# Gate and up products with high and low parts of the activations in one 512-column matmul

## The chip, the cores and the metric

The kernel runs on one core of one Trainium2 chip. The metric is the device time of one execution in microseconds (us), lower is better. Three runs of the kernel before took 1592.2, 1594.12 and 1595.83 us; their median is 1594.12 us.

## What is computed

The reference runs two small transformers one after the other on 256 tokens of width 1024. The first has two layers, each with a mixer (retention, sparse attention, a spatial gating unit) and a gated feed-forward block (FFN) of width 2816. The second has two layers with other mixers (HGRN2 with an S5 scan, latent attention) and an FFN whose gate passes a causal convolution over three tokens. Cut to the FFNs, which the change touches:

```python
# first block, both layers
gate, up = jnp.split(h @ w_gate_up[l], 2, axis=-1)
x = x + (jax.nn.silu(gate) * up) @ w_down[l]

# second block, both layers (conv over 3 tokens, per channel, plus bias)
a, u = jnp.split(hn @ w_in, 2, axis=-1)
a = conv(a, conv_w) + conv_b
return (jax.nn.silu(a) * u) @ w_out
```

All inputs are fp32.

## The kernel before

**Number format.** Most large products are made from two parts of each operand: a high part, which is the value rounded to the type fp32r (a copy by ScalarE), and a low part, which is the rest (a subtraction by VectorE). `mm3` (L512) issues three matmuls for each pair of 128x128 weights and moving columns: high x high (L514), high x low (L515) and low x high (L516), all accumulated in one place. `hTh` and `hTl` are the two parts of the normed activations, turned so that the model dimension lies on the partitions: 128 x 8 contraction blocks x 256 tokens.

**Weights.** SyncE loads weight pieces of 1 MB (2048 elements per partition) into three slots `wraw`. ScalarE writes the high part of a piece into one of three pairs `wpair` (`split_high`, L1107), VectorE the low part (`split_low`, L1624). A pair is written again when TensorE has finished with it, and a `wraw` slot is loaded again when the low part is made.

**FFN.** There are four, called by `tag` 0 to 3 below (tags 2 and 3 have the convolution). Each has 22 chunks of 128 hidden channels, two chunks in each of 11 steps. TensorE (`ffn`, L573) does in a step: `gate_up` of two chunks, and `down` of the step before. `gate_up` (L580) takes one of the four PSUM banks `work` for a chunk, gate in columns 0 to 255 and up in 256 to 511: 2 halves x 8 contraction blocks x 3 matmuls of 256 columns with the weights as stationary operand. `down` (L592) issues 24 matmuls of 512 columns into the four banks `accum`, with `hidh` and `hidl` (the two parts of the hidden activations) as stationary operand.

**ScalarE in a step** (L1149 to L1174): one split; for each chunk Silu from PSUM (L1160), or scale and bias for the convolution (L1162) and later Silu (L1166); a second split; the high parts of the hidden activations (L1172); a third split. **VectorE in a step** (L1677 to L1696): one split; for tags 2 and 3 the two other taps of the convolution, read from PSUM (L1684, L1686); the product of gate and up, with up read from PSUM (L1690), which frees the bank; a second split; the low parts of the hidden activations (L1694); a third split. Each engine works through its list in this order, waiting on semaphores.

**Beside it.** In FFN 1 GpSimd also computes the tables of the S5 scan (from L1459; the large operations are at L1544 to L1555), which are needed later. `rows` (L226) is a buffer of 128 x 2 x 1024 that no FFN uses before the final norm, except that the norms before an FFN write squares to it.

## Time and profile before

| | |
|---|---|
| median of three runs | 1594.12 us |
| span of the profiled execution | 1593.6 us |
| TensorE matmuls, busy | 1439.2 us (90%), 8688 matmuls |
| TensorE weight loads, busy | 1258.2 us (79%) |
| VectorE busy | 856.6 us (54%) |
| ScalarE busy | 618.1 us (39%) |
| GpSimd busy | 199.5 us (13%) |
| DMA | 212.06 MB, 133 GB/s on average |

The profile is one execution. Its span runs from the first to the last instruction. Busy time of an engine counts its instructions, not its waits; matmuls overlap in their pipeline, so that the sum of their durations is more than their share of the clock on the wall, and the distance between two starts is what one costs in a stream. PE is TensorE's matmuls, PEld its weight loads, DVE VectorE, ACT ScalarE, POOL GpSimd, SP SyncE. A line such as L514 is a line of the kernel. In a row, `out<-in` are the tensors written and read, and `<-` behind an idle time names what ended it.

### The profile page before, as it was taken

The page shows a single profiled execution, that of the slowest core. Times are in us where ns is not written, and L with a number is a line of the kernel's source. Part 1 is how long each engine was busy: PE and PEld are TensorE (multiplying, and loading weights), DVE is VectorE, ACT ScalarE, POOL GpSimd, SP SyncE. Part 2 cuts the span into 40 slices and gives each one's busy share as a digit, 9 for nine tenths or more (in the row PEclk, how much of TensorE's full clock was granted, in tenths as well). Part 3 has the DMA queues.
Part 4 walks back from the last instruction along what each step waited for, and adds up shares of the span by engine and source line. Part 5 has one row for each costly group of instructions (what it writes and reads, how often), then busy time and mean ns, then how long its engine had stood idle before and what let it go on. Part 6 is the DMA issues. An engine that isn't in the chain of part 4 may idle for free.

```text
span 1593.6 us, 20677 instructions
## 1 busy us (share of the span) xinstructions
PE 1439.2 (90%) x8688; PEld 1258.2 (79%) x8688; DVE 856.6 (54%) x1016; ACT 618.1 (39%) x835; POOL 199.5 (13%) x210
## 2 busy tenths in 40 slices
PE   6699999999999989799998894498999989899998
PEld 5588678999978767699997882268999876699997
DVE  4263525444456254344568658936566635466555
ACT  3322424433443233255433451025445425354543
POOL 0010000000001010004897004400000000000000
PEclk9886569999999655899999997689999999999999
DMA  7542114665543301455665330054665524456561
GB/s 251 168 121 78 32 48 141 182 187 185 181 156 80 121 27 53 93 155 181 181 190 168 108 105 0 1 159 132 197 186 174 186 67 148 115 148 184 171 198 67
DMA packets 257532, 212.06 MB, mean 133 GB/s; under 512 B 26222, under 2 KB 220031, under 8 KB 257440
## 3 DMA queue, kind: packets, MB, share of 16 engines
q1 hardware_dynamic: 244266, 206.91, 42.6%
q10 hardware_dynamic: 13174, 3.83, 1.4%
q8 instruction: 69, 1.13, 0.3%
q14 instruction: 23, 0.19, 0.0%
HBM read 208.10 MB, written 2.62 MB: 132 GB/s over the span
## 4 chain that ended last, share of the span: by engine, by line
PE 78%; DVE 10%; DMA 3%; ACT 3%; issue 2%; SPq 1%; ACTq 1%; POOL 1%; DVEq 0%; POOLq 0%
PE work L514 10%; PE accum L514 10%; PE work L516 10%; PE work L515 10%; PE accum L515 10%; PE accum L516 10%; DMA wraw<-in_w_in 3%; DVE wpair L1624 2%; PE accum L813 2%; PE work L782 2%; DVE arena L2059 2%; PE work L690 1%; PE work L564 1%; ACT wpair L1107 1%; PE work L793 1%
## 5 line engine op out<-in xcount | busy, mean ns | idle before, releaser
L1624 DVE TENSOR_TENSOR wpair<-wraw,wpair 128x2048 fp32r<-128x2048 f32 (+1 forms) x187 | 439.2, 2351 | 414.3 <-ACT wpair L1107 414.2
L1107 ACT ACTIVATE wpair<-wraw 128x2048 fp32r<-128x2048 f32 (+1 forms) x187 | 355.3, 1901 | 383.0 <-PE work L516 156.4
L514 PE MATMUL work<-hTh,wpair 128*128 128x256 f32 x1408 | 399.0, 283 | 5.9 <-DVE hTl L1632 4.9
L516 PE MATMUL work<-hTh,wpair 128*128 128x256 f32 x1408 | 398.2, 283 | 0.0
L515 PE MATMUL work<-hTl,wpair 128*128 128x256 f32 x1408 | 398.2, 283 | 0.0
L514 PEld LDWEIGHTS work<-hTh,wpair 128*128 128x128 f32 x1408 | 269.8, 192 | 8.1 <-DVE hTl L1632 6.5
L515 PEld LDWEIGHTS work<-hTl,wpair 128*128 128x128 f32 x1408 | 269.8, 192 | 2.7 <-issue 1.1
L516 PEld LDWEIGHTS work<-hTh,wpair 128*128 128x128 f32 x1408 | 269.9, 192 | 0.0
L514 PE MATMUL accum<-wpair,hTh 128*128 128x512 f32 (+2 forms) x416 | 169.6, 408 | 29.7 <-DVE wpair L1624 19.3
L1445 POOL TENSOR_SCALAR rs<-ss 128x1 f32<-128x1 f32 (+5 forms) x29 | 7.0, 241 | 1285.5 <-ACT rows L1097 919.2
L515 PE MATMUL accum<-wpair,hTh 128*128 128x512 f32 (+2 forms) x416 | 167.0, 401 | 0.0
L516 PE MATMUL accum<-wpair,hTl 128*128 128x512 f32 (+2 forms) x416 | 166.7, 401 | 0.0
L514 PE MATMUL accum<-wpair,hidh 128*128 128x512 f32 x352 | 140.2, 398 | 7.4 <-DVE hidl L1694 5.8
L515 PE MATMUL accum<-wpair,hidh 128*128 128x512 f32 x352 | 140.1, 398 | 0.0
L516 PE MATMUL accum<-wpair,hidl 128*128 128x512 f32 x352 | 140.1, 398 | 0.0
L514 PEld LDWEIGHTS accum<-wpair,hTh 128*128 128x128 f32 x416 | 86.5, 208 | 50.1 <-issue 20.7
L516 PEld LDWEIGHTS accum<-wpair,hTl 128*128 128x128 f32 x416 | 86.4, 208 | 16.3
L515 PEld LDWEIGHTS accum<-wpair,hTh 128*128 128x128 f32 x416 | 86.8, 209 | 15.2
L514 PEld LDWEIGHTS accum<-wpair,hidh 128*128 128x128 f32 x352 | 66.9, 190 | 23.0 <-DVE wpair L1624 8.5
L516 PEld LDWEIGHTS accum<-wpair,hidl 128*128 128x128 f32 x352 | 66.6, 189 | 16.1
L515 PEld LDWEIGHTS accum<-wpair,hidh 128*128 128x128 f32 x352 | 66.7, 190 | 14.3
L564 PE MATMUL work<-diag,x 128*128 128x128 f32 x256 | 40.3, 327 | 25.8 <-DVE diag L1636 25.6
(356 smaller groups left out, 1721.3 us busy)
## 6 DMA issues: line engine op xcount, KB each, us to landing
wraw<-in_w_gate_up SPq DMA_DIRECT2D x88, 512.0 KB, 5.1
wraw<-in_ffn_w_in SPq DMA_DIRECT2D x88, 512.0 KB, 5.0
wraw<-in_w_in SPq DMA_DIRECT2D x24, 1024.0 KB, 5.2
wraw<-in_w_down SPq DMA_DIRECT2D x22, 1024.0 KB, 4.9
wraw<-in_ffn_w_out SPq DMA_DIRECT2D x22, 1024.0 KB, 4.9
wraw<-in_even_w_in SPq DMA_DIRECT2D x10, 1024.0 KB, 5.2
wraw<-in_w_out SPq DMA_DIRECT2D x8, 1024.0 KB, 6.4
wraw<-in_even_w_out SPq DMA_DIRECT2D x4, 1024.0 KB, 5.1
```

What stands on the lines that cost most here:

```text
L514: mm(dst, still[0], move[0], start=start, stop=False)
L515: mm(dst, still[0], move[1], start=False, stop=False)
L516: return mm(dst, still[1], move[0], start=False, stop=stop)
L564: i = mm(b[:, k * P:(k + 1) * P], x[:, t, c:c + P], diag[:, t, :], start=True, stop=True)
L690: i = mm(b[0:HD, j * 32:j * 32 + 30], w1[:, k, :], blk[:, j, k, :], start=(k == 0), stop=(k == CMP_LEN - 1))
L782: i = mm(b[:, br * T:br * T + K], qTn[r, q, t * P:(t + 1) * P], kTn[r, br, 0:K], start=True, stop=True)
L793: i = tr(b[:, c:c + P], probs[n % 4][:, br * T + k * P:br * T + (k + 1) * P], ident[:])
L813: i = mm(banks[1 + br][:, e], pT[:, n % 3, (br * (t + 1) + k) * P:(br * (t + 1) + k + 1) * P], proj[:, k, c:c + HD], start=(k == 0), stop= ...
L1107: fn(W.pair(k)[0], W.source(k), ACT.Copy).then_inc(S["w_high"], 1)
L1445: ts(rs[0:parts, c0:c0 + n], ss[0:parts, c0:c0 + n], 1.0 / width, EPS, ALU.mult, ALU.add).then_inc(own, 1)
L1624: tt(lo, W.source(k), hi, ALU.subtract).then_inc(S["w_low"], 1)
L2059: i = v.tensor_tensor_scan(z[:, j, :], f, w[:, j, :], 0.0, ALU.mult, ALU.add)
```

## The change

The two parts of the activations now lie next to each other in one tensor `hT`, so that for one contraction block high and low parts are 512 neighbouring columns. For each chunk and half, one matmul of 512 columns multiplies the high weights with both parts (high x high into columns 0 to 255 of the bank, high x low into columns 256 to 511), and one of 256 columns adds low weights x high activations into columns 0 to 255. Each half of a chunk takes a bank of its own. VectorE then sums the two halves of each bank with a `tensor_reduce` into SBUF, the gate into `graw` and the up product into `uraw`, both views of `rows`, and that frees the bank. ScalarE, the convolution and the product read `graw` and `uraw` from there. The high parts of the hidden activations wait for a semaphore `hid_made` of their own.

```diff
-        hTh = sb("hTh", [P, KC, T], F32R)
-        hTl = sb("hTl", [P, KC, T], F32R)
+        hT = sb("hT", [P, KC, 2, T], F32R)
+        hTh, hTl = hT[:, :, 0, :], hT[:, :, 1, :]
+        graw = rows[:, 0, :].rearrange("p (f n) -> p f n", f=4)
+        uraw = rows[:, 1, :].rearrange("p (f n) -> p f n", f=4)
...
                 def gate_up(f):
 
-                    pe.wait_ge(*wk.turn())
-                    b = wk.fill(("gu", tag, f))
                     pe.wait_ge(*W.parts(("gu", tag, f)))
                     w = [m.rearrange("p (c h n) -> p c h n", c=KC, h=2) for m in W.pair()]
                     for h in range(2):
+                        pe.wait_ge(*wk.turn())
+                        b = wk.fill(("gu", tag, f, h))
                         for c in range(KC):
-                            i = mm3(b[:, h * T:(h + 1) * T], [m[:, c, h, :] for m in w], hT_at(c, slice(0, T)), c == 0, c == KC - 1)
-                    i.then_inc(*wk.fills(("gu", tag, f)))
-                    W.used(*wk.filled(("gu", tag, f)))
+                            hT_at(c, slice(0, T))
+                            mm(b, w[0][:, c, h, :], hT[:, c].rearrange("p k n -> p (k n)"), start=(c == 0), stop=False, skip_group_check=True)
+                            i = mm(b[:, 0:T], w[1][:, c, h, :], hTh[:, c, :], start=False, stop=(c == KC - 1), skip_group_check=True)
+                        i.then_inc(*wk.fills(("gu", tag, f, h)))
+                    W.used(*wk.filled(("gu", tag, f, 1)))
...
                     for f in chunks:
-                        act.wait_ge(*wk.filled(("gu", tag, f)))
-                        b = wk.bank(("gu", tag, f))
+                        act.wait_ge(*wk.freed(("gu", tag, f, 0)))
                         if f >= 4:
                             act.wait_ge(S["hid_ready"], FC * tag + f - 3)
                         if tag < 2:
-                            fn(sg[:, f % 4, :], b[:, 0:T], ACT.Silu).then_inc(S["act_silu"], 1)
+                            fn(sg[:, f % 4, :], graw[:, f % 4, :], ACT.Silu).then_inc(S["act_silu"], 1)
                         else:
-                            fn(sg[:, f % 4, :], b[:, 0:T], ACT.Identity, scale=v[:, 44 + f:45 + f], bias=v[:, 66 + f:67 + f]).then_inc(S["conv_in"], 1)
+                            fn(sg[:, f % 4, :], graw[:, f % 4, :], ACT.Identity, scale=v[:, 44 + f:45 + f], bias=v[:, 66 + f:67 + f]).then_inc(S["conv_in"], 1)
...
                     for f in chunks:
-                        act.wait_ge(*wk.freed(("gu", tag, f)))
+                        act.wait_ge(S["hid_made"], ln.next(S["hid_made"]))
...
                     split_low(1)
+                    for f in chunks:
+                        dve.wait_ge(*wk.filled(("gu", tag, f, 0)))
+                        b = wk.bank(("gu", tag, f, 0))
+                        v.tensor_reduce(graw[:, f % 4, :], b.rearrange("p (k n) -> p n k", k=2), AX_X, ALU.add).then_inc(*wk.frees(("gu", tag, f, 0)))
+                        dve.wait_ge(*wk.filled(("gu", tag, f, 1)))
+                        b = wk.bank(("gu", tag, f, 1))
+                        v.tensor_reduce(uraw[:, f % 4, :], b.rearrange("p (k n) -> p n k", k=2), AX_X, ALU.add).then_inc(*wk.frees(("gu", tag, f, 1)))
                     if tag >= 2:
                         for f in chunks:
-                            c, b = sg[:, f % 4, :], wk.bank(("gu", tag, f))
+                            c, b = sg[:, f % 4, :], graw[:, f % 4, :]
...
                     for f in chunks:
-                        b = wk.bank(("gu", tag, f))
                         dve.wait_ge(S["act_silu"], ln.next(S["act_silu"]))
-                        tt(sg[:, f % 4, :], sg[:, f % 4, :], b[:, T:2 * T], ALU.mult).then_inc(*wk.frees(("gu", tag, f)))
+                        dve.wait_ge(*wk.freed(("gu", tag, f, 1)))
+                        tt(sg[:, f % 4, :], sg[:, f % 4, :], uraw[:, f % 4, :], ALU.mult).then_inc(S["hid_made"], 1)
```

## Rows read from the trace of the kernel before

**Rows 1.** The page: busy time and share of each engine, and the chain's shares.
```profile
PE 1439.2 (90%) x8688; PEld 1258.2 (79%) x8688; DVE 856.6 (54%) x1016; ACT 618.1 (39%) x835; POOL 199.5 (13%) x210
...
PE 78%; DVE 10%; DMA 3%; ACT 3%; issue 2%; SPq 1%; ACTq 1%; POOL 1%; DVEq 0%; POOLq 0%
```

**Rows 2.** Busy time in FFNs 0 to 3 and the end of FFN 1.
```profile
252.00:443.00 191.00, 189.95 (x1330) 177.11 (x1328) 95.81 (x85) 78.39 (x81) 0.00 (x0) 1.00 0.58 177
675.00:843.00 168.00, 165.53 (x1184) 155.73 (x1183) 92.02 (x74) 78.02 (x84) 99.90 (x123) 1.00 0.59 175
1082.00:1268.00 186.00, 184.59 (x1309) 172.89 (x1307) 112.07 (x125) 89.08 (x103) 0.00 (x0) 1.00 0.58 174
1395.00:1587.00 192.00, 190.33 (x1331) 177.52 (x1330) 113.09 (x130) 88.05 (x103) 0.74 (x2) 1.00 0.52 154
860.00:877.00 17.00, 12.61 (x50) 9.81 (x49) 13.69 (x11) 3.70 (x5) 9.29 (x8) 0.90 0.75 247
```
The columns of rows 2 are: stretch, its length, then busy us (and instructions) of PE, PEld, DVE, ACT and POOL, the granted clock (1 is full), the busy share of the DMA engines and their GB/s.

**Rows 3.** Groups by line, shapes apart: busy us, mean ns, idle before.
```profile
L1624 DVE TENSOR_TENSOR wpair<-wraw,wpair 128x2048 fp32r<-128x2048 f32 x184 | 434.9, 2365 | 413.7 <-ACT wpair L1107 413.5
L514 PE MATMUL work<-hTh,wpair 128*128 128x256 f32 x1408 | 399.0, 283 | 5.9 <-DVE hTl L1632 4.9 <-issue 1.1
...
L1690 DVE TENSOR_TENSOR sg<-sg,work 128x256 f32<-128x256 f32 x88 | 36.4, 416 | 35.1 <-ACT sg L1160 30.6 <-ACT sg L1166 4.6
...
L1644 DVE TENSOR_TENSOR sg<-work,vecs 128x512 f32<-128x512 f32 x32 | 22.1, 691 | 14.0 <-PE work L564 13.4
...
L1917 DVE TENSOR_REDUCE arena<-arena 128x2 f32<-128x512 f32 x12 | 8.2, 686 | 0.4
```

**Rows 4.** Timeline of TensorE, a step of FFN 3: start us, duration us.
```profile
1455.10 0.39 PE L514 MATMUL accum<-wpair,hidh 128*128 128x512 f32 x1
...
1460.71 0.28 PE L514 MATMUL work<-hTh,wpair 128*128 128x256 f32 x1
...
1472.22 0.39 PE L514 MATMUL accum<-wpair,hidh 128*128 128x512 f32 x1
```

**Rows 5.** Timeline of TensorE, input projection of layer 0.
```profile
84.98 0.39 PE L514 MATMUL accum<-wpair,hTh 128*128 128x512 f32 x1
...
87.93 0.39 PE L515 MATMUL accum<-wpair,hTh 128*128 128x512 f32 x1
```

**Rows 6.** Timelines of ScalarE, then VectorE, in the same step of FFN 3.
```profile
1449.60 1.92 ACT L1107 ACTIVATE wpair<-wraw 128x2048 fp32r<-128x2048 f32 x1 [3.83 <-PE work L516]
...
1457.26 1.90 ACT L1107 ACTIVATE wpair<-wraw 128x2048 fp32r<-128x2048 f32 x1
...
1451.55 2.29 DVE L1624 TENSOR_TENSOR wpair<-wraw,wpair 128x2048 fp32r<-128x2048 f32 x1 [3.45 <-ACT wpair L1107]
...
1455.90 0.48 DVE L1684 SCALAR_TENSOR_TENSOR sg<-work,vecs,sg 128x255 f32<-128x255 f32 x1 [1.15 <-ACT sg L1162]
...
1459.19 2.29 DVE L1624 TENSOR_TENSOR wpair<-wraw,wpair 128x2048 fp32r<-128x2048 f32 x1 [1.39 <-ACT wpair L1107]
```

**Rows 7.** Timeline of TensorE at the end of FFN 2, first matmuls of two down products.
```profile
1262.23 0.39 PE L514 MATMUL accum<-wpair,hidh 128*128 128x512 f32 x1
...
1269.43 0.47 PE L514 MATMUL accum<-wpair,hidh 128*128 128x512 f32 x1 [1.43 <-DVE hidl L1694]
```

**Rows 8.** Lines L1690 and L1694: duration ns minimum/median/maximum, first and last start.
```profile
L1690 DVE TENSOR_TENSOR sg<-sg,work x88: 406/414/423, 264.7 to 1577.2; 128x256 f32<-128x256 f32 x88
...
L1694 DVE TENSOR_TENSOR hidl<-sg,hidh x88: 410/419/4847, 270.7 to 1578.1; 128x256 fp32r<-128x256 f32 x88
```

**Rows 9.** Timelines of GpSimd, VectorE and TensorE at the end of FFN 1.
```profile
819.32 1.91 POOL L1550 TENSOR_TENSOR arena<-arena 128x1024 f32<-128x1024 f32 x1
...
842.66 6.72 POOL L1548 TENSOR_TENSOR arena<-arena 128x2048 f32<-128x2048 f32 x1
...
844.81 8.60 DVE L1694 TENSOR_TENSOR hidl<-sg,hidh 128x256 fp32r<-128x256 f32 x2
...
869.36 0.47 PE L514 MATMUL accum<-wpair,hidh 128*128 128x512 f32 x1 [4.39 <-DVE hidl L1694]
```

More of the change, by code:

```diff
@@ L439, in build @@
           cmp_scores cmp_exp cmp_probs cmp_turned gates_ready gm_rows silu_ready mixed
-          act_silu hid_high hid_ready down_done conv_in conv_done
+          act_silu hid_made hid_high hid_ready down_done conv_in conv_done
           s5_dt s5_arg s5_trig lb_arg lb_exp s5_tables s5_pad s5_wT table_done
```

## Prediction, made before the changed kernel was run

> **What bounds the kernel now.** I read the page's busy shares and its chain first. TensorE is busy for 90% of the span and holds 78% of the chain that ended last [rows 1], so TensorE is the first suspect. The stretches of the four feed-forward blocks (FFNs), cut out of the span, sharpen this: in each, TensorE is busy for over 98% of the stretch at full granted clock, while VectorE is busy for 50 to 60% [rows 2]. The groups by line say what the time is: 1408 matmuls of each of the three kinds of the gate and up product, 256 columns each [rows 3]. Their 283 ns of mean duration overlap, so a duration is not a cost here. The cost is the distance from start to start, and it is read from the timeline. In FFN 3, 24 down matmuls of 512 columns lie between 1455.10 and 1460.71, and 96 gate-up matmuls of 256 columns between 1460.71 and 1472.22 [rows 4]: 5.61/24 = 233.8 ns and 11.51/96 = 119.9 ns, with no gap. So one step of an FFN (two chunks and one down product) is 17.1 us of unbroken TensorE work, and what shortens a matmul there shortens the span, as long as VectorE and ScalarE keep up.
>
> **Part 1: two matmuls become one.** For each chunk, half and contraction block, three matmuls of 256 columns (359.7 ns) become one of 512 and one of 256. The number of columns is the same, so only what a matmul costs beside its columns is saved. For 512 columns the trace has two prices. The down product pays 233.8 ns [rows 4]. The input projection of layer 0 runs 13 distances between 84.98 and 87.93 [rows 5], 226.9 ns each. I take 226.9, because those matmuls use the same two tensors as the changed ones (hTh and wpair), while the down product has hidh and hidl as stationary operand; at 256 columns nothing suggests that it matters which of the two tensors moves. The new pair is then 226.9 + 119.9 = 346.8 ns, 12.9 ns less; with the down product's price it is 353.7 ns, 6.0 ns less. There are 1408 triples, 352 per FFN: 18.2 us in all, 4.5 per FFN, or at the other end 8.5 and 2.1. A third of these weight loads goes too, but they lie beside the matmuls already and I cost them at nothing.
>
> **Part 2: VectorE sums the halves.** Added are 4 reduces a step, 176 in all, each reading 512 elements per partition from PSUM. No such form is in the trace. The nearest is the reduce of 512 elements in SBUF, 686 ns [rows 3]. From below, a 128x256 operation with a PSUM input is 414 ns [rows 3], if output elements counted instead of input elements. From above, twice the nearest row, 1.37 us, if the stride of 256 elements between the two summed values halves the read rate. I take 0.69 us, 0.63 from start to start as neighbours overlap: 2.5 us a step. Nothing is saved against it: the product at L1690 stays, with an SBUF operand.
>
> Where do they go? They stand behind the first weight split of the step and in front of everything else, and four waits for filled banks stand there; the convolution, the products, the second split and the low parts of hid queue behind them. Take the end of the first chunk as t = 0, from the step in FFN 3 [rows 6]. ScalarE's high part of the split starts at 0.3 us and VectorE's low part ends at 4.5. The reduces run 4.5 to 7.0 (the fourth needs only the second chunk, which ends at 5.55). The convolutions, twice 0.48 us a chunk and 1.0 with the wait between them, end at 9.0, the last Silu at 9.4, the second split's high part (1.9) at 11.3, its low part (2.3) at 13.5. TensorE needs that pair when the second chunk of the next step starts, at 5.55 + 5.61 + 5.55 = 16.7. Slack 3.2 us, so in the steady state I cost the reduces at nothing; that cover is gone when one reduce takes over 0.63 + 3.2/4 = 1.4 us. In FFNs 0 and 1 there is no convolution and the slack is about 5.7 us. The banks (four, now two per chunk) are free at 5.1 to 7.0, before TensorE comes back to them at 11.2. The third split (down weights) ends at about 16.5, needed at 22.3. SyncE's loads follow the splits by up to 2 us later than now; each has over 5 us before its split.
>
> **Part 3: the ends of the FFNs.** After the last chunk only one down product (5.6 us) covers the chain, not three. In FFN 2 that chain already ends last: the last chunk ended at 1262.23 and the last down product began at 1269.43, after a wait of 1.43 us for hidl [rows 7], 7.2 us after. With the reduces, the fourth ends 1.4 us after the chunk, both convolutions come behind it, hidh's high parts wait for the later product, and hidl comes at about 8.8: 1.6 us more. In FFN 0 without a convolution hidl comes at 6.2 against 5.6 needed, but the additions behind it are held by the last split as now: 0.1 us. In FFN 3 no splits are left, hidl comes at 5.2: nothing.
>
> **Part 4: FFN 1, where GpSimd works too.** This is the largest unknown. The product at L1690 now reads one operand from PSUM and takes 406 to 423 ns in all 88 cases; hidl's subtraction at L1694 reads two from SBUF, takes 419 in the median, and once 4847 [rows 8]. That one began at 844.81, under a GpSimd table operation that began at 842.66 and ran for 6.72 us, and two of them took 8.60 us; TensorE then waited 4.39 us for hidl at 869.36 [rows 9]. After the change the product reads sg and uraw, both in SBUF, so in FFN 1 two more VectorE operations a step can be caught like this. The table operations of 2048 elements lie in the last two steps only. There I laid the order out anew: split, reduces, product behind one GpSimd operation, the next product behind the next one (about 4.4 us each when not held itself: 6.72 less the 2.3 us of the split that was in front), then split, two subtractions. The split for the last chunk ends some 5.5 us after TensorE wants it, the low part of that step's hid and its down weights come at about 863.7, the last down product starts near 872 against 869.36 now. After such waits the granted clock is below full (0.90 in that stretch [rows 2]), which adds up to 1.5 us. So FFN 1 gives back its 4.5 us and ends about 2 us later than now. Bounds: if the products slip between the table operations, the 4.5 us stay; if each catches a further one, it ends 6 us later.
> The Trainium skill states the same as a rule (SBUF — State Buffer, Who interferes with whom): a VectorE operation with two SBUF inputs contends with GpSimd, and whoever holds the shared port blocks the other, while a reduce on this chip never does. The 4847 ns agree; that the reduces stay free, no run here shows. Without the rule FFN 1 would save its 4.5 us.
>
> **Sum.** FFN 0: -4.5 + 0.1. FFN 1: +2. FFN 2: -4.5 + 1.6. FFN 3: -4.5. Together -9.8 us on the profiled span of 1593.6, so 1583.8. The median of the runs shown, 1594.12, is 0.5 us above that span, so the forecast is 1584.3.
>
> **The rivals.**
> A. The 512-column matmul costs here what it costs in the same step, 233.8 ns. For: the down product stands beside it, with the same ScalarE, VectorE and DMA activity. Against: the operands differ, and the projections run at 226.9. It gives FFN 0 -2.0, FFN 1 +3, FFN 2 -0.5, FFN 3 -2.1: -1.6, 1592.5.
> The Trainium skill (TensorE: Matmul & The Clock Gate, Back-to-back issue gap) gives N/2.4 + 2.5 ns for an isolated stream, so that a merged pair would save 2.5 ns: 3.5 us in all as an estimate of that page, near rival A. The trace does not agree, as its 256 columns take 119.9 ns and not 109.
> B. Slower: the reduce reads PSUM so slowly that it ends last. From 1.4 us each, what is above it is paid four times in each of the 20 steps of FFNs 2 and 3. At three times the nearest row (2.06 us) that is 2.6 us x 20 = 53 us, less the 10 saved: about 1637. Against: an operation on 128x512 with a PSUM input takes 691 ns, no more than the reduce from SBUF [rows 3].
> C. GpSimd and VectorE catch each other in more than the last two steps of FFN 1, from which hid and splits come late by 3 us a step in the five steps with wide table operations: +15 on FFN 1 instead of +2, 1597.3. Against: before the last two steps the table operations are half as long or less (1.91 us for one of 1024 elements [rows 9]), and the slack is 5.7 us.
> D. The products slip through, FFN 1 saves 4.5 us: 1577.8.
>
> **How the numbers follow.** Forecast 0.57 (1580 to 1588), A 0.19, B 0.05, C 0.07, D 0.12. What a measurement can tell from no change is about 0.2%, 3.2 us. Forecast and D are faster: 0.69. A is the same, with a part of it either side: 0.18. B, C and a rest of A are slower: 0.13. The range takes in D and A with the profile's scatter: 1577 to 1595, leaving out B, C and the far ends.
>
> **What would show it.** The timeline inside a chunk: distances of 227 and 120 ns alternating (forecast), or 234 and 120 (A). The reduce's mean: 0.69 us; no wait of TensorE for wpair in FFNs 0, 2 and 3. In FFN 2 the wait for hidl grows from 1.4 to about 3 us, less with slower matmuls. In FFN 1 L1690's successor has a maximum of several us, and TensorE waits for a split before the last chunk. If that product never exceeds 0.5 us, part 4 is wrong; if TensorE waits in every step of FFNs 2 and 3, part 2 is.

## The result, and the profile after

The changed kernel took 1591.18 us (median of 20 runs) beside 1595.78 us of the kernel before (20 runs, on the same chip): ratio 0.9963, 95% interval 0.9945 to 0.9981, so 5.9 us faster, with 3.0 to 8.8 in the interval. That is faster by more than the 0.2% that can be told from no change. The forecast was 9.8 us, the range holds the measured time, and the size is off: the forecast's 9.8 lie beyond the interval's end.

The page of the changed kernel (the lines that answer to [rows 1] and [rows 3]; the groups read busy us, mean ns, idle before):

```profile
span 1585.4 us, 18125 instructions
PE 1432.2 (90%) x7280; PEld 1185.3 (75%) x7280; DVE 963.0 (61%) x1192; ACT 627.2 (40%) x835; POOL 200.0 (13%) x210
L591 PE MATMUL work<-hT,wpair 128*128 128x512 f32 x1408 | 497.0, 396 | 9.7 <-DVE hT L1635 5.7
L592 PE MATMUL work<-hT,wpair 128*128 128x256 f32 x1408 | 395.3, 281 | 0.0
L1686 DVE TENSOR_REDUCE rows<-work 128x256 f32<-128x512 f32 x88 | 59.9, 681 | 0.0
L1689 DVE TENSOR_REDUCE rows<-work 128x256 f32<-128x512 f32 x88 | 59.8, 679 | 0.0
```

L591 is the merged matmul, L592 the 256-column one that is left, L1686 and L1689 are the sums. TensorE has 1408 matmuls fewer and is as busy as before in share, so it still sets the pace. Where did the time go? The four FFNs, from the start of the first gate-up matmul to the start of the last down matmul, in the profile of the changed kernel:

```profile
252.16:438.21 186.05, 185.26 (x967) 157.28 (x968) 120.04 (x127) 79.98 (x81) 0.00 (x0) 1.00 0.60 181
669.45:868.27 198.82, 189.12 (x967) 159.69 (x968) 150.77 (x127) 88.53 (x92) 125.83 (x133) 0.98 0.57 172
1075.55:1264.02 188.47, 185.26 (x968) 157.11 (x968) 139.67 (x171) 93.97 (x107) 0.20 (x2) 1.00 0.59 180
1392.14:1577.69 185.55, 185.04 (x968) 157.35 (x968) 135.26 (x169) 89.70 (x102) 0.26 (x2) 1.00 0.52 159
```

The columns are those of rows 2. Cut in the same way, the kernel before has 188.97, 198.21, 190.63 and 188.97 us. So FFN 0 gained 2.9 us, FFN 1 lost 0.6, FFN 2 gained 2.2, FFN 3 gained 3.4: 7.9 in all. The stages between the FFNs differ too, by 4.3 us less to 6.0 us more, though no instruction of theirs was edited: between FFN 0 and FFN 1 the profiles of the kernel before and of the four kernels below that keep three matmuls show 231.0 to 237.0 us, those of the nine with the merged one 228.2 to 232.9 (means 234.3 and 230.2). If those 4 us belonged to the change in every run, the timed gain would be near 12 us, and its interval ends at 8.8. What they are stays open. Below, I compare the sum of the four FFNs, beside the timed ratio.

What a pair costs is read from the start of a step's gate-up product to the start of the down product behind it, 32 pairs. Two steps of FFN 0 in a row:

```profile
297.78 0.40 PE L591 MATMUL work<-hT,wpair 128*128 128x512 f32 x1
308.89 0.39 PE L516 MATMUL accum<-wpair,hidh 128*128 128x512 f32 x1
314.51 0.39 PE L591 MATMUL work<-hT,wpair 128*128 128x512 f32 x1
325.80 0.40 PE L516 MATMUL accum<-wpair,hidh 128*128 128x512 f32 x1
```

11.11/32 = 347.2 ns in the first, 11.29/32 = 352.8 ns in the second. These are close to the two sums that the prediction had as alternatives (346.8 and 353.7), and they take turns, step by step, in all four FFNs; the down product always pays 5.62/24 = 234 ns. Nothing waits in these steps. Within a pair the split is another than forecast: from the start of a 512-column matmul to the next start it is 230.1 ns on average in the first product shown and 236.2 in the products at the high price, and behind the 256-column one 116.9 and 116.5. So no pair is 227 + 120 or 234 + 120; only the pair's sum is.

Which step gets which price is not fixed by the program. The gate-up product of FFN 0 that took 11.11 us above took 11.29 in the kernel below with the tables two steps earlier, which differs from the changed one only in when ScalarE does some work of FFN 1:

```profile
299.49 0.39 PE L591 MATMUL work<-hT,wpair 128*128 128x512 f32 x1
310.78 0.40 PE L516 MATMUL accum<-wpair,hidh 128*128 128x512 f32 x1
```

The two prices took turns in all four FFNs of all six profiled kernels that keep the changed kernel's matmuls, their order and the place of their operands (the changed one, and of those below the sum in PSUM, the wide operations left out, the tables earlier, the doubling in halves and the doubling moved).

The end of FFN 1 in the changed kernel: TensorE, then VectorE, then GpSimd (brackets: idle us before, and what ended it; "x2" is two operations shown as one row).

```profile
842.76 0.50 PE L591 MATMUL work<-hT,wpair 128*128 128x512 f32 x1 [3.95 <-DVE wpair L1627]
853.46 0.50 PE L516 MATMUL accum<-wpair,hidh 128*128 128x512 f32 x1 [3.30 <-DVE wpair L1627]
862.82 0.47 PE L516 MATMUL accum<-wpair,hidh 128*128 128x512 f32 x1 [1.93 <-DVE hidl L1704]
...
830.89 6.20 DVE L1700 TENSOR_TENSOR sg<-sg,rows 128x256 f32<-128x256 f32 x2
837.01 5.69 DVE L1627 TENSOR_TENSOR wpair<-wraw,wpair 128x2048 fp32r<-128x2048 f32 x1
842.63 8.55 DVE L1704 TENSOR_TENSOR hidl<-sg,hidh 128x256 fp32r<-128x256 f32 x2
...
832.12 4.68 POOL L1551 TENSOR_TENSOR arena<-arena 128x2048 f32<-128x2048 f32 x1
836.89 3.67 POOL L1553 TENSOR_TENSOR arena<-arena 128x2048 f32<-128x2048 f32 x1
840.64 5.54 POOL L1555 TENSOR_TENSOR arena<-arena 128x2048 f32<-128x2048 f32 x1
```

VectorE's operations with two SBUF operands wait for the GpSimd operation that runs and then take their own time: the pair of products, about 0.4 us each elsewhere, takes 6.20 us and ends at 837.09, after L1551 has ended at 836.80; the split, 2.29 us elsewhere, takes 5.69 and ends 2.1 us after L1553. Three waits of TensorE stand beside them, 9.2 us. The kernel before had two, 6.0 us: 4.39 for hidl [rows 9] and this one for a split:

```profile
859.09 0.50 PE L514 MATMUL accum<-wpair,hidh 128*128 128x512 f32 x1 [1.62 <-DVE wpair L1624]
```

The splits were thus held in the kernel before already: two in a row took 5.70 and 6.70 us there, from 853.34 on. And the last down product of FFN 1, which comes behind the last wait, ran at a lower granted clock (the number in front of the DMA share) in the kernel before and at the full one in the changed kernel, which hides 1.5 us (first the kernel before, then the changed one):

```profile
869.36:876.35 6.99, 6.99 (x23) 5.57 (x24) 3.69 (x4) 1.15 (x2) 0.20 (x2) 0.76 0.98 333
862.82:868.27 5.45, 5.45 (x23) 4.40 (x24) 3.91 (x4) 1.22 (x3) 0.20 (x2) 1.00 0.95 283
```

### The profile page after: what moved, and what is told of

Its sections match the earlier page's. It is cut to its first block, busy times and chain, and to the rows that moved or that the text cites. A ratio compares the mean times of both kernels' runs of the same rounds, so it can differ in the third digit from the quotient of the medians.

```text
span 1585.4 us, 18125 instructions
## 1 busy us (share of the span) xinstructions
PE 1432.2 (90%) x7280; PEld 1185.3 (75%) x7280; DVE 963.0 (61%) x1192; ACT 627.2 (40%) x835; POOL 200.0 (13%) x210
## 3 DMA queue, kind: packets, MB, share of 16 engines
HBM read 208.10 MB, written 2.62 MB: 133 GB/s over the span
## 4 chain that ended last, share of the span: by engine, by line
PE 78%; DVE 11%; DMA 3%; ACT 3%; issue 2%; ACTq 1%; POOL 1%; SPq 0%; DVEq 0%; POOLq 0%
PE work L591 19%; PE accum L516 10%; PE accum L517 10%; PE accum L518 10%; PE work L592 10%; DMA bias_line<-arena 3%; PE accum L817 2%; DVE wpair L1627 2%; PE work L786 2%; DVE arena L2069 2%; ACT wpair L1111 1%; PE work L566 1%; PE work L694 1%; PE work L797 1%; PE accum L810 1%
## 5 line engine op out<-in xcount | busy, mean ns | idle before, releaser
L1627 DVE TENSOR_TENSOR wpair<-wraw,wpair 128x2048 fp32r<-128x2048 f32 (+1 forms) x187 | 434.8, 2327 | 360.8 <-ACT wpair L1111 360.6
L591 PE MATMUL work<-hT,wpair 128*128 128x512 f32 x1408 | 497.0, 396 | 9.7 <-DVE hT L1635 5.7
L592 PE MATMUL work<-hT,wpair 128*128 128x256 f32 x1408 | 395.3, 281 | 0.0
L591 PEld LDWEIGHTS work<-hT,wpair 128*128 128x128 f32 x1408 | 264.7, 188 | 73.9 <-DVE hT L1635 7.8
L592 PEld LDWEIGHTS work<-hT,wpair 128*128 128x128 f32 x1408 | 266.7, 189 | 1.6
L516 PE MATMUL accum<-wpair,hT 128*128 128x512 f32 (+2 forms) x416 | 171.4, 412 | 25.6 <-DVE wpair L1627 15.3
L517 PE MATMUL accum<-wpair,hT 128*128 128x512 f32 (+2 forms) x416 | 168.2, 404 | 0.0
L518 PE MATMUL accum<-wpair,hT 128*128 128x512 f32 (+2 forms) x416 | 167.7, 403 | 0.0
L516 PEld LDWEIGHTS accum<-wpair,hT 128*128 128x128 f32 x416 | 87.0, 209 | 46.6 <-issue 14.7
L518 PEld LDWEIGHTS accum<-wpair,hT 128*128 128x128 f32 x416 | 87.2, 210 | 16.6
L517 PEld LDWEIGHTS accum<-wpair,hT 128*128 128x128 f32 x416 | 87.5, 210 | 15.7
L1686 DVE TENSOR_REDUCE rows<-work 128x256 f32<-128x512 f32 x88 | 59.9, 681 | 0.0
L1689 DVE TENSOR_REDUCE rows<-work 128x256 f32<-128x512 f32 x88 | 59.8, 679 | 0.0
```

Of the source, the lines that this page charges most:

```text
L516: mm(dst, still[0], move[0], start=start, stop=False)
L517: mm(dst, still[0], move[1], start=False, stop=False)
L518: return mm(dst, still[1], move[0], start=False, stop=stop)
L591: mm(b, w[0][:, c, h, :], hT[:, c].rearrange("p k n -> p (k n)"), start=(c == 0), stop=False, skip_group_check=True)
L592: i = mm(b[:, 0:T], w[1][:, c, h, :], hTh[:, c, :], start=False, stop=(c == KC - 1), skip_group_check=True)
L1627: tt(lo, W.source(k), hi, ALU.subtract).then_inc(S["w_low"], 1)
```

## The experiments

All are timed beside the kernel before; a difference in us is the ratio's, on 1598 to 1599 us. "FFNs" is the sum of the four stretches above in the profile (before 766.8, changed 758.9).

**The merged matmul alone taken back.**

```diff
-mm(b, w[0][:, c, h, :], hT[:, c].rearrange("p k n -> p (k n)"), start=(c == 0), stop=False, skip_group_check=True)
+mm(b[:, 0:T], w[0][:, c, h, :], hTh[:, c, :], start=(c == 0), stop=False, skip_group_check=True)
+mm(b[:, T:2 * T], w[0][:, c, h, :], hTl[:, c, :], start=False, stop=False, skip_group_check=True)
```

> The change without its one merged matmul: bank per half chunk, the sums on VectorE and all its waits stay as in the changed kernel, but each triple is again three matmuls of 256 columns (high x high, high x low, low x high), so each costs 3 x 119.9 = 359.7 ns instead of 346 to 355 ns. Theory M (the merged matmul alone carries the gain, TensorE bounds the FFNs): the gate and up products take 11.5 us in a step again, 1408 x about 9.6 ns = 13.5 us more than the changed kernel, which was 5.9 us below the kernel before; so about 7.6 us above the kernel before, ratio 1.005, and no step of FFN 0, 2 or 3 under 17.1 us. Rival V (the change gains by its banks and its sums, which free or fill something earlier, or VectorE sets the pace): within 2 us of the changed kernel, ratio 0.995 to 0.998.

Measured: ratio 1.0049 (1.0025 to 1.0073), 7.8 us above the kernel before; FFNs 771.6. A step's gate-up product takes 11.50 us again:

```profile
299.54 0.28 PE L591 MATMUL work<-hT,wpair 128*128 128x256 f32 x1
311.04 0.39 PE L516 MATMUL accum<-wpair,hidh 128*128 128x512 f32 x1
```

Theory M holds: 7.8 us for 7.6, closer than the interval (4.0 to 11.7) can show. The merged matmul brings 12.7 us in the FFNs (771.6 less 758.9) and 13.7 in time by the two ratios; everything else in the change costs 4.8 in the FFNs, of which 3.3 in FFN 1 (201.47 for 198.21) and 1.2 in FFN 2.

**One matmul more in a step.** `half` is true for the last matmul of a down product, `c` is 256.

```diff
+if half:
+    mm(dst[:, 0:c], still[1], move[0][:, 0:c], start=False, stop=False, skip_group_check=True)
+    return mm(dst[:, c:], still[1], move[0][:, c:], start=False, stop=False, skip_group_check=True)
```

> The changed kernel's 512-column gate-up matmul costs 227 ns in one step and 234 ns in the next, in turn. This kernel is the changed one with one edit: in each down product but an FFN's last, the last of the 24 matmuls of 512 columns is issued as two of 256 columns, so a step has 89 matmuls in place of 88 (+6 ns each, 40 times: 0.2 us). Theory S (the two prices are a state of TensorE that lasts over a product and that the number or kind of the matmuls before it sets): the pattern changes: all steps at 11.1 us of gate-up (about 18 steps x 0.18 = 3.3 us faster than the changed kernel), all at 11.3 us (3.3 us slower), or another period. Rival B (the price goes with what repeats every second step of the program, such as the four buffers of the hidden activations that are written beside it): the same pattern, 11.1 and 11.3 us in turn, and the same time within 0.5 us.

Measured: ratio 0.998 (0.9959 to 1.0002), FFNs 764.7. In FFNs 0, 2 and 3 every step pays the high price; in FFN 1 the two still take turns. Two successive steps of FFN 0 (L595 is the merged matmul):

```profile
283.32 0.40 PE L595 MATMUL work<-hT,wpair 128*128 128x512 f32 x1
294.61 0.39 PE L516 MATMUL accum<-wpair,hidh 128*128 128x512 f32 x1
300.23 0.39 PE L595 MATMUL work<-hT,wpair 128*128 128x512 f32 x1
311.53 0.40 PE L516 MATMUL accum<-wpair,hidh 128*128 128x512 f32 x1
```

Rival B falls: nothing that repeats every second step was touched, and the pattern changed; that the changed kernel's own FFN 0 starts with the high price and its FFN 1 with the low one says the same. That what ran before sets the price (theory S) is borne out; a rule that gives all four FFNs is not. Of the 5.8 us more in the FFNs than the changed kernel's, 3 are not the price: the last down products of FFNs 1 and 2 ran at a mean granted clock of 0.76, 7.00 us each for 5.46.

**The hidden activations at another address.** `hidh` and `hidl` are allocated right behind `hT` instead of behind the small tensors; only addresses change. With them everything allocated between the two places moves by 8 KB per partition, `wpair`, which the gate-up product reads, among it.

> The changed kernel with the two tensors of the hidden activations (stationary in the down product) allocated right behind the normalized activations: only addresses in SBUF move. Theory A (the down product's matmul of 512 columns costs 234 ns and not 227 because of where its stationary operand lies): down products fall from 5.62 to 5.45 us, 44 x 0.17 = 7.3 us off the time. Rival S (a state of TensorE, nothing to do with addresses): 5.62 us stays, the time is that of the changed kernel within its uncertainty, though the turn of fast and slow steps may shift.

Measured: ratio 0.9963 (0.9938 to 0.9988), as the changed kernel; FFNs 758.1. But the profile is that of neither theory:

```profile
295.22 0.40 PE L516 MATMUL accum<-wpair,hidh 128*128 128x512 f32 x1
300.72 0.39 PE L591 MATMUL work<-hT,wpair 128*128 128x512 f32 x1
312.01 0.40 PE L516 MATMUL accum<-wpair,hidh 128*128 128x512 f32 x1
```

The down product takes 5.50 us, 0.12 less, in all steps but an FFN's first (5.45 to 5.48); its first eleven distances are 224 to 241 ns, 232 on average, and the later ones 227. The gate-up product takes 11.29 in all steps, where it took 11.29 and 11.11 in turn. So addresses move the prices of both products, and the total stays within 0.8 us in the FFNs. Which tensor's address does it is not shown, since `wpair` moved too.

**The two matmuls of a pair in the other order.**

```diff
-mm(b, w[0][:, c, h, :], hT[:, c].rearrange("p k n -> p (k n)"), start=(c == 0), stop=False, skip_group_check=True)
-i = mm(b[:, 0:T], w[1][:, c, h, :], hTh[:, c, :], start=False, stop=(c == KC - 1), skip_group_check=True)
+mm(b[:, 0:T], w[1][:, c, h, :], hTh[:, c, :], start=(c == 0), stop=False, skip_group_check=True)
+i = mm(b, w[0][:, c, h, :], hT[:, c].rearrange("p k n -> p (k n)"), start=False, stop=(c == KC - 1), skip_group_check=True)
```

> The changed kernel with the two matmuls of each pair in the other order: the 256 columns of low weights x high activations first, then the 512 columns. Same work. Theory S (the pair's price is a state of TensorE that outlasts the pair: 346.8 or 353.7 ns whatever the order): gate-up products of a step still take 11.1 us in some steps and 11.3 in others, and the time is that of the changed kernel within 2 us. Rival F (the second read of the same activations right behind the first, or the writes of 512 columns after 256 in the bank, set the price): one price in all steps, 11.1 us (3.3 us faster) or another.

Measured: ratio 0.9967 (0.9947 to 0.9988); FFNs 764.0, 5.1 more than the changed kernel's. One price in the steps of all four FFNs, 11.30 or 11.31 us: rival F's pattern, at the high end. Of the 5.1 us, 1.5 are the last down product of FFN 2, at a mean granted clock of 0.76 (7.00 us for 5.46). The timed ratio cannot tell this kernel from the changed one. The order matters too, then.

**The sum of the up half in PSUM.** `g` is the gate's bank. The waits of ScalarE and VectorE follow the new order of events (not shown).

```diff
-v.tensor_reduce(uraw[:, f % 4, :], b.rearrange("p (k n) -> p n k", k=2), AX_X, ALU.add).then_inc(*wk.frees(("gu", tag, f, 1)))
+v.tensor_reduce(g[:, 0:T], b.rearrange("p (k n) -> p n k", k=2), AX_X, ALU.add).then_inc(*wk.frees(("gu", tag, f, 1)))
-tt(sg[:, f % 4, :], sg[:, f % 4, :], uraw[:, f % 4, :], ALU.mult).then_inc(S["hid_made"], 1)
+tt(sg[:, f % 4, :], sg[:, f % 4, :], wk.bank(("gu", tag, f, 0))[:, 0:T], ALU.mult).then_inc(*wk.frees(("gu", tag, f, 0)))
```

> The changed kernel with the sum of the up half written to PSUM, over the gate's bank (which its reduce has read), in place of SBUF. The product silu x up again reads one operand from SBUF and one from PSUM, as in the kernel before; the gate's bank comes free with the product, the up's bank with its sum. Theory P (beside GpSimd's wide tables in FFN 1 the product of two SBUF operands waits for the port that both engines share: 4.83 us for one of them, and a chain of such waits behind it): products back to 0.41 to 0.42 us, FFN 1 is 2 to 4 us shorter (195 to 197 us where the changed kernel has 199.1), FFNs 0, 2 and 3 unchanged within 0.5 us, the whole 2 to 4 us under the changed kernel. Rival Q (the split of the last weight pieces, which reads two SBUF operands in both kernels, sets FFN 1's end whatever the product does): product short, FFN 1 within 1 us of 199.1. Rival R (the gate's bank is held too long): TensorE waits at the start of a gate-up product in every step, some 40 times 0.3 us or more, slower.

Measured: ratio 1.0054 (1.003 to 1.0078), 8.6 us slower than before; FFNs 780.6. The product (L1701), the split and hidl's subtraction (L1705) at the end of FFN 1, then two waits of TensorE:

```profile
838.46 0.74 DVE L1701 TENSOR_TENSOR sg<-sg,work 128x256 f32<-128x256 f32 x2
840.04 6.03 DVE L1627 TENSOR_TENSOR wpair<-wraw,wpair 128x2048 fp32r<-128x2048 f32 x1 [0.84 <-ACT wpair L1111]
845.99 7.58 DVE L1705 TENSOR_TENSOR hidl<-sg,hidh 128x256 fp32r<-128x256 f32 x2
...
860.13 0.80 PE L516 MATMUL accum<-wpair,hidh 128*128 128x512 f32 x1 [7.78 <-DVE wpair L1627]
...
1421.22 0.77 PE L591 MATMUL work<-hT,wpair 128*128 128x512 f32 x1 [3.89 <-DVE sg L1701]
```

The product is never held now, as theory P has it, and FFN 1 gains nothing: the next operation with two SBUF operands is held in its place (rival Q). TensorE's two waits at the end, 7.78 and 2.18 us, are 10.0 where the changed kernel has 9.2. The last row is rival R, but only once an FFN (2.06 to 3.89 us): step 1 follows step 0 with no down product between them, the four banks are just one step of gate-up, and a bank held until the product is not free by then. FFN 1's first two gate-up products took 26.98 us instead of 23.48; without these 3.5 us its 202.9 are 199.4, the changed kernel's 198.8.

**GpSimd's wide operations left out, in both kernels.** All six operations of a doubling go over `m` columns.

```diff
+m = min(n, 4)
-A, B = etmp[0][:, :, 0:n], etmp[1][:, :, 0:n]
+A, B = etmp[0][:, :, 0:m], etmp[1][:, :, 0:m]
```

> The changed kernel with GpSimd's tables of cosines and sines in FFN 1 mostly left out: each of the eight doublings computes at most 4 new columns of each table (a memset fills the rest), so the output is not the reference's, and GpSimd has no wide operation in the last steps of FFN 1. Theory P (FFN 1's missing gain is the port that VectorE and GpSimd share: VectorE's two-operand operations wait there for GpSimd's wide ones): no VectorE operation of 4 us or more in FFN 1, the two waits of TensorE for the split and the one for the hidden activations (3.95, 3.30, 1.93 us) gone, FFN 1 at 189 to 190 us as FFN 0 (188.4) where the changed kernel has 199.1, so some 9 us under the changed kernel's time, 15 under the kernel before. Rival O (VectorE's own order: reduces ahead of the split make the split late, with or without GpSimd): FFN 1 stays above 196 us.

> The kernel before with the same part of GpSimd's tables left out (output not the reference's). Its FFN 1 took 198.4 us beside GpSimd's wide operations, its FFN 0 191.8. Theory P (the same port, less of it since its product has one operand from PSUM): FFN 1 falls to 192 to 193 us, so 5 to 6 us under the kernel before. Then the change is worth about 3 to 3.5 us in FFN 1 when GpSimd is quiet, as in the other three FFNs, and the two short kernels stand 11 to 13 us apart, where the full ones stand 5.9 (8.4 in the sum of the four FFNs of the two profiles). Rival O (the change's own price in FFN 1 comes from VectorE's longer chain there): the two short kernels stand as far apart as the full ones.

Measured: 0.9862 (0.9835 to 0.9888) and 0.9949 (0.9931 to 0.9968), so 22.1 and 8.2 us under the kernel before. FFN 1 without the wide operations, kernel before and changed kernel:

```profile
677.89:867.95 190.06, 188.61 (x1320) 176.23 (x1320) 95.99 (x82) 85.57 (x90) 73.05 (x131) 1.00 0.58 178
...
671.42:857.79 186.37, 185.49 (x968) 157.34 (x968) 123.36 (x127) 87.64 (x91) 75.34 (x131) 1.00 0.60 181
```

The wide operations cost the kernel before 8.2 us in FFN 1 (198.2 less 190.1) and the changed one 12.5 (198.8 less 186.4); TensorE's waits at the end are 6.0 and 9.2 of these, and the rest goes with matmuls at a lower granted clock beside the waits. Without the wide operations the change brings 3.7 us there. About 1 us of that is not the matmuls: in FFN 1's second gate-up product the kernel before waits 1.05 us (0.95 in the short one) for nothing that the profile shows, as all five profiled kernels with three matmuls do and none with the merged one. Rival O falls: the changed kernel's FFN 1 takes 186.4 us, not over 196, and the two short kernels stand 13.9 us apart by the ratios (11.2 in the FFNs), not 5.9 (7.9).

**The tables two steps earlier, in both kernels.**

```diff
-if s == 2:
+if s == 0:
...
-if s == 4:
+if s == 2:
```

> The changed kernel with ScalarE's two groups of steps for the tables issued two FFN steps earlier (step 0 and 2 of FFN 1 in place of 2 and 4), so GpSimd's wide operations run about 34 us earlier and end some 30 us before FFN 1 does. Nothing is left out. Theory P: VectorE's operations are held as long as before, but in steps in which TensorE has weights and hidden activations in hand for several us; the waits at the end of FFN 1 go, FFN 1 at 189 to 193 us, the whole 6 to 9 us under the changed kernel. Rival E (the held operations add up to more than the slack wherever they stand: the waits only move to the steps before): FFN 1 at 196 to 200 us, the whole within 2 us of the changed kernel.

> The kernel before with the same edit as early_tables: ScalarE's steps for GpSimd's tables two FFN steps earlier, nothing left out. Theory P: FFN 1 goes from 198.4 to 192 or 193 us, the whole 5 to 6 us under the kernel before, and the changed kernel keeps its gain of about 3.4 us in each of FFN 0, 1 and 3 against this one. Rival E: no change within 2 us.

Measured: the changed kernel with it 0.9988 (0.9971 to 1.0004), some 4 us worse than without, FFN 1 204.9 us; the kernel before with it 0.9968 (0.9947 to 0.9989), 5.1 better than without, FFN 1 192.8. The waits in FFN 1, first of the changed kernel, then of the kernel before:

```profile
690.86 0.77 PE L591 MATMUL work<-hT,wpair 128*128 128x512 f32 x1 [5.59 <-DVE rows L1686]
820.33 0.79 PE L591 MATMUL work<-hT,wpair 128*128 128x512 f32 x1 [3.70 <-DVE wpair L1627]
831.03 0.50 PE L516 MATMUL accum<-wpair,hidh 128*128 128x512 f32 x1 [2.50 <-DVE wpair L1627]
...
826.11 0.50 PE L514 MATMUL accum<-wpair,hidh 128*128 128x512 f32 x1 [1.62 <-DVE wpair L1624]
832.82 0.36 PE L514 MATMUL work<-hTh,wpair 128*128 128x256 f32 x1 [0.83 <-DVE wpair L1624]
```

The same edit, two answers. In the middle of the FFN the kernel before covers the holds but for 2.5 us (theory P); the changed one, whose VectorE has the sums to do as well, still waits 6.2 (rival E). The first row is a cost that I had not seen: ScalarE waited for the tables' parameters from memory until 685.63, the split behind it and then the sums came late, and with them the banks. In the kernel before, which needs one bank a chunk and not two, ScalarE waited just as long for them and TensorE did not wait.

**The last doubling cut in halves.** Six operations of 2048 elements become twelve of 1024, in place.

> The changed kernel with each of the six operations of GpSimd's last doubling done as two of 1024 elements (where they were, nothing left out). Theory L (VectorE is held until the GpSimd operation that runs ends, so a hold is as long as that operation): holds of at most 3.8 us where they were up to 5.7, FFN 1 3 to 6 us shorter than the 198.8 of the changed kernel, first to last matmul. Rival T (the two engines take turns, and the same work on both costs the same however it is cut, or more, since GpSimd's part lasts longer): FFN 1 within 1.5 us of 198.8 or above.

Measured: ratio 0.9935 (0.9914 to 0.9956), 10.4 us under the kernel before; FFN 1 197.0 us, FFN 2 190.1, FFNs 758.9. The longest product fell from 4.83 to 2.62 us, yet FFN 1 gained 1.8 us only, and hidl's wait at its end is 8.03 us: TensorE's waits there add up to 9.5 us where they were 9.2. Between theory L and rival T, nearer to T. FFN 2 took 1.6 us more, 1.3 of it in its last down product (6.74 us for 5.46, mean granted clock 0.79), behind a wait as long as in the changed kernel (2.78 and 2.70), so the edit does not explain it. By its FFNs this kernel is equal to the changed one; the timed intervals overlap.

**The last doubling behind FFN 1, in both kernels.** `last_doubling` does the same six operations over 512 elements, four times, with its temporaries in `late`.

```diff
-while n < T:
+while 2 * n < T:
...
 norm()
+last_doubling()
```

> The changed kernel with GpSimd's last doubling of the tables (six operations of 2048 elements, 28 us from 822.8 on, in FFN 1's last two steps) moved behind the norm that follows FFN 1, as 24 operations of 512 elements, into the 80 us in which GpSimd is idle there (873 to 954 us); its temporaries lie in the space of the later states, and VectorE's wait for the tables moves ahead of those. Nothing is left out. Theory P: the waits of 3.95, 3.30 and 1.93 us at FFN 1's end go, FFN 1 (first to last matmul) from 198.8 to 186.5 to 190 us; VectorE's splits in the next stage are held by 1 us or so each and TensorE waits there 0 to 3 us more; the whole 6 to 11 us under the changed kernel, 12 to 17 under the kernel before. Rival N (the contention moves with the operations: the next stage's projections wait for their splits as FFN 1 did): FFN 1 short, the stage behind it 6 us or more longer, the whole within 3 us of the changed kernel.

> The kernel before with the same edit as late_after, nothing left out. Theory P: FFN 1 (first to last matmul) from 198.2 to 190 to 192 us, the whole 4 to 8 us under the kernel before; the change is then worth 3 to 4 us in FFN 1, as in FFN 0, 2 and 3, and late_after stands 10 to 14 us under this kernel by the profiles' FFNs. Rival N: within 2 us of the kernel before.

Measured: 0.9871 (0.9847 to 0.9895) for the changed kernel with it, median 1578.41 us, 20.6 us under the kernel before; 0.9976 (0.9956 to 0.9996) for the kernel before with it, 3.8 us under it. FFN 1 in both, changed first, and the first of the moved operations beside the longest:

```profile
670.13:856.49 186.36, 185.48 (x967) 157.29 (x968) 131.90 (x127) 87.77 (x91) 93.10 (x121) 1.00 0.60 181
...
672.43:862.67 190.24, 188.59 (x1319) 176.23 (x1320) 103.31 (x82) 85.63 (x90) 90.61 (x121) 1.00 0.59 177
...
859.86 1.04 POOL L1579 TENSOR_TENSOR arena<-arena 128x512 f32<-128x512 f32 x1
879.78 3.22 POOL L1583 TENSOR_TENSOR arena<-arena 128x512 f32<-128x512 f32 x1
```

FFN 1 is as short as without the wide operations, and rival N falls: the moved operations end at 898 us, long before VectorE first reads their tables at 946, and the splits of that stage take at most 3.03 us in the changed kernel and 3.27 in the kernel before, with no wait of TensorE for them. The stage between FFN 1 and FFN 2 took 2.9 and 3.8 us more than without the move, not the 6 of rival N; the kernels before with the tables left out or earlier, which run nothing of this there, took 3.5 and 3.0 more too. The FFNs sum to 746.7 us, 20.1 less than before, and the ratio says 20.6. This version beats both kernels: 14.7 us under the changed one by the two ratios, with nothing left out. For the kernel before, the FFNs gained 8.0 us and the ratio says 3.8 (0.6 to 7.0); the rest is open. With the move in both kernels the FFNs of the changed one are 12.1 us shorter (758.8 less 746.7), where they were 7.9 without it.

## Why the prediction was right or wrong

**The bound** was right: the merged matmul carries the gain (13.7 us are lost when it alone is taken back), and no step of FFNs 0, 2 or 3 waits between the first and the last down product. For FFN 1 the prediction read TensorE's busy share from a stretch that ends at 843 us [rows 2], before the waits; from the first matmul to the last down product it is 96% (190.64 of 198.21 us), not over 98%.

**Part 1, the term that was mis-sized.** It took 12.9 ns for a triple from the projection's 226.9 ns. Measured are 359.4 ns (11.50/32) less 347.2 and less 352.8 in turn: 12.2 and 6.6, mean 9.4, so 3.3 us an FFN and not 4.5 (FFN 3 shows 3.4). Both prices stood in the trace of before, and the step that failed is the choice between them by operand. The address run shows that addresses have a part in it, the run with one more matmul that they are not the whole of it, and the swapped one that the order counts; why stays open. The forecast's pair and rival A's were each right in about half the steps, as sums: the distances inside a pair, 230 and 117 ns or 236 and 117, are neither's. That the measured mean lies between the two is luck as far as the prediction goes: it had no step in which they take turns.
The Trainium skill's isolated gap (TensorE: Matmul & The Clock Gate, Back-to-back issue gap), 2.5 ns saved a pair as an estimate of that page, is not what the rows show, and the page says itself that a stream of weight loads and matmuls is spaced otherwise. The 3.5 us that the prediction has from it are before the costs of parts 2 to 4, so they belong beside rival A's 8.5 us and not beside its net 1.6.

**Part 2** was right: the sums take 0.68 us beside the 0.69 assumed, and no steady step waits. What it left out is what the two banks a chunk take away. It asked only whether the banks are free in a normal step. With four banks and two a chunk TensorE can run one step ahead, where it had two, and the two kernels that made VectorE late once (the held gate bank, the early tables) paid at the first step, where no down product lies between.

**Part 3** was right: in FFN 2 the wait for hidl grew from 1.43 to 2.70 us (forecast 3.0, less with slower matmuls):

```profile
1258.56 0.47 PE L516 MATMUL accum<-wpair,hidh 128*128 128x512 f32 x1 [2.70 <-DVE hidl L1704]
```

FFN 2 therefore gained 2.2 where FFN 3 gained 3.4. FFN 0 has a wait of 0.28 us for hidl at its end, near the 0.1 assumed.

**Part 4** was right in what would happen and in where: a product of 4.83 us, splits late before the last chunk and before its down weights, hid late behind them. The first wait is 3.95 us for 5.5. The last down product begins at 862.82; FFN 1 began 8.69 us earlier than before, which makes it 871.5 on the old clock, for a forecast of 872. FFN 1 ended 0.6 us longer, for a forecast of 2; the start of the last down product was 2.1 us later than before, and its 5.45 us at full granted clock, for 6.99 at 0.76 in the kernel before, hide 1.5 of that. So the near hit of the start is the mechanism's, and the end came out better by the clock. Two things were missed. The prediction took the splits in the kernel before as not held; they were, up to 6.70 us. And the reason given was not the whole one: that the product came to have two SBUF operands. With one operand back in PSUM, the split and hidl's subtraction were held instead. Summed over FFN 1, what these operations took above their medians is 24.9 us in the kernel before, 30.7 in the changed one and 21.7 with the sum in PSUM: there VectorE is held less than in the kernel before, and TensorE still waits 10.0 us for 6.0. What is left as the cause is that VectorE has the sums to do in the same steps in which it is held, so there is less slack to absorb the holds: 8.2 us of cost became 12.5. This is argued from what the other runs leave; no run took the sums alone away. The faster gate-up product, which leaves VectorE less time, has a small part: with three matmuls again the waits are 8.2 us, not 9.2.
The Trainium skill's rule on the shared port (SBUF — State Buffer, Who interferes with whom) has it that a reduce is never blocked by GpSimd on this chip. The trace agrees for these sums, which read PSUM: all 176, those beside the wide operations too, took between 673 and 685 ns. A reduce that reads SBUF beside GpSimd is in no row here.

**The sum.** Forecast -4.4, +2, -2.9 and -4.5; the FFNs show -2.9, +0.6, -2.2 and -3.4. The price of the pair takes about 1.2 us from each; FFN 1 came out 1.4 better in spite of it; the total is -7.9 for -9.8. The interval of the timed -5.9 holds -7.9. Rivals B, C and D did not occur.

## What to carry to other kernels

Price a merged matmul by every distance that the trace has for its size, and where there are two do not choose by the operands alone. Before adding work to VectorE, look for the stretch in which GpSimd has wide operations on SBUF: slack that is idle elsewhere is used up there, and making one operation immune moves the hold to the next. The cure was not to reshape VectorE's work but to move GpSimd's into its idle time: on top of the change that was worth more (14.7 us by the ratios, 12.2 in the FFNs) than the change itself, and less without the change (3.8 and 8.0). When a profile's stages are compared, look at the granted clock of the stretch behind a wait: after waits of 2.6 to 3.1 us at the end of FFN 2 it was full in seven of the ten profiles with VectorE's sums and a mean of 0.76 to 0.79 in three, worth 1.3 to 1.5 us each time, with no edit to explain it.

## What the runs showed of the hardware

- A stream of matmuls of 512 columns at full granted clock goes at 227 or at 234 ns from start to start, mostly over whole products. Pairs of 512 and 256 columns go at 347 or 353 ns, with 230 or 236 ns behind the 512 columns and 117 behind the 256; a stream of 256 columns alone goes at 120 ns. Which of the two holds for a pair changed with the number of matmuls in a step, with addresses in SBUF and with the order within a pair, and where it alternates the same product had one price in one kernel's profile and the other in the next. Why is open.
- A held operation of VectorE ends after the GpSimd operation that runs, whatever its own size: 4.83 us for one of 0.41, 5.69 for one of 2.29. GpSimd is held as well: its operations of 512 elements took from 1.04 to 3.22 us, the 3.22 shown beside a split of VectorE. Halving GpSimd's operations nearly halved the longest hold of a product (4.83 to 2.62 us), and brought FFN 1 only 1.8 us.
